# The last expert tile and the final norm, worked by halves of the output columns

## The reference

```
def moe_swiglu(h, router, w_in, w_out):
    ...
    for e in range(N_EXPERTS):
        y = y + gates[:, e:e + 1].astype(hf.dtype) * swiglu(hf, w_in[e], w_out[e])
    return y.reshape(B, S, D)
...
        x = x + g_f[:, None, :] * y
...
    return rms_norm(x, final_norm)
```

## Time and profile before

| | us |
|---|---|
| median of three runs | 1626.99 (1626.41 to 1627.26) |
| the profiled execution's own time | 1628.95 |
| its span | 1626.9 |
| TensorE busy | 1555.2 |
| VectorE busy | 1425.9 |
| ScalarE busy | 1085.1 |

### The profile page before, as it was taken

One profiled execution on the slowest core, in us unless ns is written; L12 is line 12 of the kernel. 1 busy time (PEld: TensorE's weight loads), 2 busy tenths in 40 slices (PEclk: granted clock), 3 DMA queues, 4 the chain that ended last, 5 costly groups with the idle time before them and its releaser, 6 DMA issues.

```text
span 1626.9 us, 22949 instructions
## 1 busy us (share of the span) xinstructions
PE 1555.2 (96%) x7341; PEld 1288.8 (79%) x7341; DVE 1425.9 (88%) x1604; ACT 1085.1 (67%) x1224; POOL 61.6 (4%) x47
## 2 busy tenths in 40 slices
PE   4999998999989998999999999999999999999996
PEld 4788776888869776888888888888888888888884
DVE  6989989788788766989989989989989999999995
ACT  2554445434456546878778778778778778778874
POOL 0222300000000110000000000000000000000000
PEclk8999999999999998999999999999999999999998
DMA  9977776888856423999999999999999999999992
GB/s 323 348 257 267 266 248 227 276 310 292 313 195 233 155 80 120 391 380 333 373 370 338 362 389 329 370 370 340 363 381 337 368 371 343 365 383 334 356 378 82
DMA packets 235114, 500.91 MB, mean 308 GB/s; under 512 B 9744, under 2 KB 40640, under 8 KB 235072
## 3 DMA queue, kind: packets, MB, share of 16 engines
q1 hardware_dynamic: 233904, 500.29, 84.8%
q10 hardware_dynamic: 1168, 0.07, 0.1%
HBM read 499.28 MB, written 1.05 MB: 308 GB/s over the span
## 4 chain that ended last, share of the span: by engine, by line
PE 79%; DVE 11%; DMA 4%; issue 3%; ACT 2%; SPq 0%; DVEq 0%; ACTq 0%
PE ps L500 23%; PE ps L502 23%; PE ps L501 23%; DMA ada<-in_ada_w 4%; DVE acc L1483 3%; DVE w_lo L1464 3%; PE ps L994 2%; PE ps L784 1%; PE ps L786 1%; PE ps L788 1%; PE ps L1027 1%; PE ps L1003 1%; PE ps L1028 0%; PE ps L1004 0%; PE ps L1011 0%
## 5 line engine op out<-in xcount | busy, mean ns | idle before, releaser
L1464 DVE TENSOR_TENSOR w_lo<-raw,w_hi 128x1024 fp32r<-128x1024 f32 x834 | 995.7, 1234 | 66.2 <-ACT w_hi L1094 54.0
L1094 ACT ACTIVATE w_hi<-raw 128x1024 fp32r<-128x1024 f32 x834 | 860.9, 1057 | 210.2 <-PE ps L502 183.3
L500 PE MATMUL ps<-w_hi,RA 128*128 128x512 f32 x1528 | 606.3, 397 | 9.8 <-DVE w_lo L1464 3.5
L502 PE MATMUL ps<-w_hi,RA 128*128 128x512 f32 x1528 | 597.3, 391 | 0.0
L501 PE MATMUL ps<-w_lo,RA 128*128 128x512 f32 x1528 | 596.3, 390 | 0.0
L500 PEld LDWEIGHTS ps<-w_hi,RA 128*128 128x128 f32 x1528 | 287.7, 188 | 69.3 <-DVE w_lo L1464 4.2
L502 PEld LDWEIGHTS ps<-w_hi,RA 128*128 128x128 f32 x1528 | 287.5, 188 | 61.3
L501 PEld LDWEIGHTS ps<-w_lo,RA 128*128 128x128 f32 x1528 | 288.0, 188 | 58.2 <-issue 0.7
L500 PE MATMUL ps<-w_hi,hT_hi 128*128 128x512 f32 x400 | 160.6, 402 | 6.0 <-issue 4.0
L1483 DVE SCALAR_TENSOR_TENSOR acc<-ada,cond,acc 128x512 f32<-128x512 f32 x189 | 154.0, 815 | 4.2 <-DMA ada<-in_ada_w 1.2
L501 PE MATMUL ps<-w_lo,hT_hi 128*128 128x512 f32 x400 | 157.2, 393 | 0.0
(11 more groups left out here) (253 smaller groups left out, 1030.5 us busy)
## 6 DMA issues: line engine op xcount, KB each, us to landing
raw<-in_moe_w_in SPq DMA_DIRECT2D x224, 1024.0 KB
raw<-in_moe_w_out SPq DMA_DIRECT2D x112, 1024.0 KB
ada<-in_ada_w SPq DMA_DIRECT2D x46, 1024.0 KB, 7.3
raw<-in_ff_w_in SPq DMA_DIRECT2D x44, 512.0 KB
raw<-in_ret_w_in SPq DMA_DIRECT2D x16, 1024.0 KB
raw<-in_ff_w_out SPq DMA_DIRECT2D x11, 1024.0 KB
raw<-in_ret_w_in SPq DMA_DIRECT2D x16, 512.0 KB
raw<-in_ret_w_out SPq DMA_DIRECT2D x8, 1024.0 KB
```

Of the source, the lines that this page charges most:

```text
L500: pe.matmul(out, a_hi, b_hi, start=first, stop=False)
L502: return pe.matmul(out, a_lo, b_hi, start=False, stop=last)
L1094: act.activation(w_hi[:, cn % RING, cols], raw[:, cn % RAW, cols], ACT.Copy).then_inc(hi_done, 1)
L1464: v.tensor_tensor(w_lo[:, cn % RING, cols], raw[:, cn % RAW, cols], w_hi[:, cn % RING, cols].bitcast(f32), ALU.subtract).then_inc(lo_done, 1)
```

## The change

Five things are changed, all of them at the end of the last expert and behind it.
- In the last step (j = 6, `more=False`) quarters 12 to 15 are split in front of `tile_high` on ScalarE and between `tile_product` and `tile_low` on VectorE; the two `split` calls behind the steps go.
- The last `down` becomes `down_by_columns`: the 12 matmuls of output columns 0 to 511 (bank 4) first, then the 12 of columns 512 to 1023 (bank 5).
- Gate, high part and low part are made for each half of the columns, with semaphores of their own for the first half.
- `scatter_by_columns` makes both blocks of the first half, then both of the second; the accumulation is four instructions of 128 x 512.
- The squares are four of 128 x 512. The first half's sum, divided by D and with EPS added, becomes the bias of the root (a new VectorE instruction behind the loop), whose input is the second half's sum.

```diff
+            def down_by_columns(c, m, n, p):
+
+                pe.wait_ge(eTl_ok, n + 1)
+                for k in range(2):
+                    for h in range(2):
+                        s = (c + h) % RING
+                        for t in range(2):
+                            if k == 0:
+                                landed(c + h, m, t)
+                            kc, cols = 2 * h + t, slice(t * D + k * TW, t * D + (k + 1) * TW)
+                            last = passes(ps[:, 4 + k, :], eT_hi[:, kc, :], eT_lo[:, kc, :], w_hi[:, s, cols],
+                                          w_lo[:, s, cols], False, kc == 3)
+                            if k == 1:
+                                last.then_inc(w_used, 1)
+                    if k == 0:
+                        last.then_inc(down_h, 1)
+
+            def scatter_by_columns(ne, p):
+
+                pe.wait_ge(hotT_ok, ne + 1)
+                for n in range(2):
+                    if n == 0:
+                        pe.wait_ge(yl_h, p + 1)
+                    else:
+                        pe.wait_ge(yl_ok, ne + 1)
+                    for b in range(NB):
+                        o, cols = ps[:, 6 - 2 * b + n, :], slice(n * TW, (n + 1) * TW)
+                        pe.matmul(o, hotT[:, b * P:(b + 1) * P], y_hi[:, cols], start=True, stop=False)
+                        last = pe.matmul(o, hotT[:, b * P:(b + 1) * P], y_lo[:, cols], start=False, stop=True)
+                        last.then_inc(scat_done if n else scat_h, 1)
...
-                down(U_MOE + MOE_U - 2, me, me + (ET - 1), False, True)
-                scatter(ne)
+                down_by_columns(U_MOE + MOE_U - 2, me, me + (ET - 1), p)
+                scatter_by_columns(ne, p)
...
@@ scalar: step, and the end
-                if j < ET - 1 or more:
+                if j == ET - 1 and not more:
+                    split_quarters(c, me, 12, 16)
+                else:
                     split_quarters(c, me, 12, 14)
...
-                split(U_MOE + MOE_U - 2, me)
-                split(U_MOE + MOE_U - 1, me)
-                y_high(ne)
+                act.wait_ge(yg_h, p + 1)
+                act.activation(y_hi[:, 0:TW], y32[:, 0:TW], ACT.Copy).then_inc(yh_h, 1)
+                act.wait_ge(yg_ok, ne + 1)
+                act.activation(y_hi[:, TW:D], y32[:, TW:D], ACT.Copy).then_inc(yh_ok, 1)
 
             root_table()
-            for b in range(NB):
-                root_mean_square(4, b)
+            for k in range(2):
+                for b in range(NB):
+                    if k == 0:
+                        act.wait_ge(yacc_h[b], npass)
+                    elif b == 0:
+                        act.wait_ge(yacc_a, npass)
+                    else:
+                        act.wait_ge(yacc_ok, NB * NE * npass)
+                    cols = slice(k * TW, (k + 1) * TW)
+                    act.activation(xn[:, b, cols], x[:, b, cols], ACT.Square,
+                                   accum_out=stat[:, 20 + 2 * k + b:21 + 2 * k + b]).then_inc(ssh_ok, 1)
+                    if k == 1:
+                        act.wait_ge(ssh_ok, NB + b + 1)
+                        act.wait_ge(bias_ok, 1)
+                        act.activation(stat[:, 4 + b:5 + b], stat[:, 22 + b:23 + b], ACT.Sqrt, bias=stat[:, 50 + b:51 + b],
+                                       scale=1.0 / D).then_inc(rs_ok, 1)
...
@@ vector: step, and the end
-                if j < ET - 1 or more:
+                if j == ET - 1 and not more:
+                    split_quarters(c, me, 12, 16)
+                else:
                     split_quarters(c, me, 13, 14)
...
-                split(U_MOE + MOE_U - 2, me)
-                split(U_MOE + MOE_U - 1, me)
-                y_gated(ne, U_MOE + MOE_U, me)
-                y_low(ne)
-                accumulate(ne, NE - 1)
+                for k in range(2):
+                    cols = slice(k * TW, (k + 1) * TW)
+                    if k == 0:
+                        dve.wait_ge(down_h, p + 1)
+                    else:
+                        dve.wait_ge(w_used, before_half(U_MOE + MOE_U, me))
+                    v.tensor_tensor(y32[:, cols], ps[:, 4 + k, :], gate_f[:, cols], ALU.mult).then_inc(yg_ok if k else yg_h, 1)
+                    if k == 0:
+                        dve.wait_ge(yh_h, p + 1)
+                    else:
+                        dve.wait_ge(yh_ok, ne + 1)
+                    v.tensor_tensor(y_lo[:, cols], y32[:, cols], y_hi[:, cols].bitcast(f32),
+                                    ALU.subtract).then_inc(yl_ok if k else yl_h, 1)
+                for k in range(2):
+                    cols = slice(k * TW, (k + 1) * TW)
+                    for b in range(NB):
+                        if k == 0:
+                            dve.wait_ge(scat_h, NB * p + (b + 1))
+                        else:
+                            dve.wait_ge(scat_done, NB * ne + (b + 1))
+                        ins = v.scalar_tensor_tensor(x[:, b, cols], ps[:, 6 - 2 * b + k, :], gate_e[:, b, NE - 1:NE], x[:, b, cols],
+                                                     ALU.mult, ALU.add)
...
                 steps.link(v.tensor_scalar(slot, slot, -float(P), None, ALU.add))
                 steps.leave(npass)
 
 
+            dve.wait_ge(ssh_ok, NB)
+            v.tensor_scalar(stat[:, 50:52], stat[:, 20:22], 1.0 / D, EPS, ALU.mult, ALU.add).then_inc(bias_ok, 1)
             dve.wait_ge(fnorm_in, 16)
```

More of the change, by code:

```diff
@@ L233, in trunk @@
         yl_ok = sem("yl_ok"); scat_done = sem("scat_done")
+        down_h = sem("down_h"); yg_h = sem("yg_h"); yh_h = sem("yh_h"); yl_h = sem("yl_h"); scat_h = sem("scat_h")
+        yacc_h = [sem(f"yacc_h{b}") for b in range(NB)]; yacc_a = sem("yacc_a"); ssh_ok = sem("ssh_ok"); bias_ok = sem("bias_ok")
         o_ok = sem("o_ok"); stored = sem("stored")
@@ L1996, in _ @@
                     step(j, me, ne, NE - 1, more=False)
-                split(U_MOE + MOE_U - 2, me)
-                split(U_MOE + MOE_U - 1, me)
-                y_gated(ne, U_MOE + MOE_U, me)
-                y_low(ne)
-                accumulate(ne, NE - 1)
+                for k in range(2):
[20 more added lines that the diff above has]
+                                                     ALU.mult, ALU.add)
+                        if k == 0:
+                            ins.then_inc(yacc_h[b], 1)
+                        elif b == 0:
+                            ins.then_inc(yacc_a, 1)
+                        else:
+                            ins.then_inc(yacc_ok, NB)
                 steps.link(v.tensor_scalar(slot, slot, -float(P), None, ALU.add))
                 steps.leave(npass)
+            dve.wait_ge(ssh_ok, NB)
+            v.tensor_scalar(stat[:, 50:52], stat[:, 20:22], 1.0 / D, EPS, ALU.mult, ALU.add).then_inc(bias_ok, 1)
             dve.wait_ge(fnorm_in, 16)
```

## The result

| | before | changed |
|---|---|---|
| median of the first comparison (six runs each), us | 1626.2 | 1617.66 |
| lowest to highest | 1625.14 to 1627.26 | 1616.53 to 1621.12 |
| profiled execution, its span | 1626.9 | 1619.1 |
| from the start of the last tile_high to the end of the span | 24.9 | 18.9 |

The ratio is 0.995 (95% interval 0.9937 to 0.9963), a gain of 8.5 us between the medians. Forecast were 1620.9 us, range 1620.1 to 1623.0, a gain of 6.1. The profiled spans differ by 7.8 us, and the trace splits that in two: 1.8 us lie ahead of the last tile_high, which starts at 1600.20 instead of 1601.98, and 6.0 us behind it.

The account below looks back on a forecast made before the run. The prediction took the last 25 us as a chain where all engines wait for one another; 1.48 + 1.51 + 2.49 + 0.65 = 6.1 us off the median 1626.99 gives 1620.9 us, range 1620.1 to 1623.0.

Parts of the forecast that it names:

- 1 early split: Before the last down projection: quarters 12 to 15 split early, so the product waits for tile_low alone; gain 1.48 us.
- 2 halves to the low part: Last product, gate, high and low part by column halves, the first half beside matmuls; gain 1.51 us.
- 3 scatter and sums: Scatter by halves at full clock, four half-wide accumulations on VectorE 0.66 us apart; gain 2.49 us.
- 4 squares, bias: Final norm: squares by halves, root waiting for a bias on VectorE behind the loop's exit; gain 0.65 us.
- behind the root: Scaling and store at the end: from the first root on all stays as now.
- the gain carries over to the median: Whole run: the span's 6.1 us gain taken off the median of the runs, 1626.99, giving 1620.9 us.
- theory A: Posed after the first result: the program's front varies by chance per execution, and six runs drew a short one.
- VectorE's order: Rival, chance 0.05: low part 0 queued before gate 1 takes the overlap; 1622.8 us, 1623.0 with hand-offs.
- A stall for code: Rival, chance 0.04: a 3.2 us issue stall at the loop's exit on VectorE; 1624.1 us.
- Half clock in the last product: Rival: TensorE at half clock in the last down projection; code and clock together 0.07 for same time.
- The early split does nothing: Rival, chance 0.02: the quarters split early wait for something late; 1622.4 us.
- Slower: Rival, chance 0.03: weights land late, so quarter 15 delays tile_high and all behind; say 1631 us.

Follow-up runs that it names:

- experiment 3: Changed kernel with the early split undone, the last four quarters again split behind tile_high and tile_low: 1621.3 us, ratio 0.998 to the kernel before.
- experiment 1: Kernel before with only the change's new semaphores declared and never used: 1624.43 us against 1624.69, ratio 0.9996.
- experiment 2: Kernel before with the early split of the last four quarters alone: 1622.41 us, ratio 0.9986 to the kernel before.
- Experiments 4 and 10: Changed kernel unaltered, run again twice against the kernel before: 1619.42 us against 1624.69, ratio 0.9967; then 1617.52 us against 1623.59, ratio 0.9964.
- experiment 9: Changed kernel loading a quarter of each modulation weight block, testing transfer landing against TensorE's early clock as source of scatter: 1616.37 us, 1613.16 to 1617.12.
- experiment 7: Changed kernel with the last product by rows of weights again, all else by halves: 1621.55 us in one run.

## Why the prediction was right in the end stretch and wrong in the total
The terms, all from the first trace of each kernel:

| | forecast | measured | how |
|---|---|---|---|
| 1 early split | 1.48 | 1.40 | tile_high to product: 2.86 to 1.46 |
| 2 halves to the low part | 1.51 | 1.55 | product's start to low part's end: 9.39 to 7.84 |
| 3 scatter and sums | 2.49 | 2.50 | to the last accumulation's end: 5.14 to 2.64 |
| 4 squares, bias | 0.65 | 0.67 | to the root: 1.22 to 0.55 |
| behind the root | 0 | -0.10 | 6.31 to 6.41 |
| sum | 6.1 | 6.0 | 24.9 to 18.9 |

*The four steps held.* The fixed cost that the rule against small instructions names (the Trainium skill, VectorE: DVE Perf Modes, on the errata) is there: two half-wide low parts take 1.38 us, a whole one 1.23. The first of them is covered. In part 1 ScalarE's last quarter starts 3.16 us ahead of tile_high, as forecast (3.18), but the product starts 0.14 behind tile_low instead of 0.05 ("issue" 0.12 on the chain). Where a quarter of weights released it, before and in experiment 3, it was 0.05. Why tile_low costs 0.09 more was not tested. In part 2 the overlap was complete. In part 3 the half-wide accumulation takes 0.74 and follows each 0.66, as estimated, and VectorE binds, not TensorE; the scatter had full clock. In part 4 the loop's exit costs nothing beyond its instructions: the bias starts 0.21 behind the slot update and the root waits for it, 0.46 us. That the sum came within 0.1 us is in part luck: 2.49 took the scatter's clock from one trace, in which it was half throughout. Measured against experiment 1's trace of the same end, the stretch gains 5.7 us, and against experiment 2's with its 1.40 added back, 5.5.

*The step that failed is the last one, "the gain carries over to the median" with "0.4 for the spread of runs".* I took the median of three runs, 1626.99, as the kernel's time, and their spread of 0.85 us as its scatter. The same kernel then ran 57 times more, from 1620.83 to 1628.61. Three runs had drawn the slow side: the mean over all 60 is 1624.85 us, 2.1 less than my starting value. The changed kernel's 16 runs have a mean of 1618.46. Starting from 1624.85, the forecast gain of 6.1 gives 1618.75. So the absolute time was 3.2 us off (1620.9 against 1617.66): 2.1 for the start, 0.3 because the gain between the means is 6.4 and not 6.1, and 0.8 because the median of the six runs lies below the mean of all 16. The gains measured in three comparisons, 8.5, 5.3 and 6.1 us, have the 6.0 us of the trace in their midst, and the mean over all runs gives 6.4, give or take 0.8 (twice the standard error). In the traces, too, the start of the last tile_high doesn't tell the kernels apart: 1596.9 to 1602.0 in four with the end whole, 1596.0 to 1600.2 in eight with it by halves. All this supports theory A. Experiments 4 and 10 show that the 8.5 us don't come back, while a systematic part of up to some 1.5 us in front of the end is not excluded. The chip is not what scatters: the three later comparisons were made on three different chips, and within each the kernel before spreads over 7.1, 7.8 and 5.8 us. What makes the front scatter stays open, since experiment 9 confirmed neither explanation.

The same step also took the time outside the span as fixed, 2.05 us. It is 1.7 to 2.4 us in the 54 runs of the kernel before that have their span on record (1.8 in the mean) and 2.0 to 3.2 in the 16 of the changed one (2.3). This goes against the gain by 0.5 us, so it can't be why the measured time came out lower.

*My range should have been wider on both sides*, by half the spread of the kernel's runs, some 4 us, since three runs don't tell from which side they were drawn, and the statement that 0.2% can be told from no change holds only for many runs: with 5 to 12 runs against 11 to 29 the intervals were 0.0019 to 0.0031 wide, 3 to 5 us.

*The rivals.* VectorE's order: did not come, and experiment 7 shows it would have cost 1.3 us with a lead of 0.68 us. A stall for code: none, the exit costs 0.21 us in all; the Trainium skill's rule (Runtime: NRT & Kernel Launch, Instruction fetch mechanics), which puts such stalls on taken branches, agrees. Half clock in the last product: not in the changed kernel, though experiment 3 shows it where the long gap stays in front. The early split does nothing: it gives 1.40 at its own place, and without it the gain up to the root falls from 6.1 to 2.4 us. Slower: the weights had landed, as ScalarE's quarters show, which waited for matmuls only, 0.3 us at most.

## What to carry to other kernels
A chain through three engines at the end of a program can be folded by halves at the price of the fixed cost of each instruction (0.15 to 0.20 us here: 0.69 twice against 1.23 for the low part, 0.74 twice against 1.28 for the accumulation), if the producer delivers the first half early; the order of the columns in the last product was worth 1.3 us, and it only works when that product no longer waits for its weights. Keep TensorE's idle gaps short: 0.8 to 1.4 us of the gain was its clock, depending on the trace. And before a gain of some us in 1600 is read off whole runs, look at how far the runs of one kernel scatter; a stretch within one trace, from a common event to the end, told each part to 0.1 us with a single run, except where TensorE's clock differed from trace to trace.

## What the runs showed that I had not expected
- The same program takes from 1620.8 to 1628.6 us (60 runs), and in the traces most of the scatter arises in the first 225 us; three runs in a row lay within 0.85.
- TensorE's clock behind a gap of 3.6 to 3.7 us: at half through eight matmuls (first trace), back at full for the last two (experiment 1), full for the first 0.8 us and half afterwards (experiment 2). Behind a gap of 2.9 us: full in three traces, at half from the seventh matmul on and full again 2.7 us later in another (experiment 3). A gap of this length has no single price.
- GpSimd starts a small instruction 0.08 us behind the one it waits for after 1007 us of rest, and needs 0.19 us for it.
